# One decoder step on one core: the delta rule's sample stage takes in the gated norm behind it, and the attention's outputs use other PSUM banks

## The reference

```python
# odd layer: one input projection, two head groups, one output projection
o_dn, s_dn = delta_rule(dq, dk, dv, gdec, beta, s_dn)     # 4 heads of 128; one state of 128 x 128 per sample and head
o_dn = rmsnorm(o_dn, dn_norm) * silu(dz)                  # per head, over its 128 features: the gated norm
out = concat([o_sb, o_dn]) @ w_out

# every layer: cross-attention to 256 memory rows, 4 heads of 256
s = q @ mk.T * 256 ** -0.5
o = softmax(s) @ mv                                        # the outputs
x += o @ w_xo
```

## Time and profile before

| | us |
|---|---|
| three runs: median (lowest to highest) | 2115.48 (2109.58 to 2116.85) |
| the profiled execution, its own time | 2111.75 |
| its span, first to last instruction | 2110.0 |
| TensorE busy | 1979.2 (94%) |
| VectorE busy | 1194.9 (57%) |
| ScalarE busy | 504.4 (24%) |
| GpSimd busy | 231.5 (11%) |

### The profile page before, as it was taken

The page is one execution under the profiler, slowest core; times in us unless marked ns, Lnnn a source line. Parts: engine busy times, 40 slices in busy tenths (PEclk is TensorE's granted clock), DMA queues, the critical chain, the costliest instruction groups (busy, mean ns, idle before and its releaser), DMA issues. The chain is left out here.

```text
span 2110.0 us, 40071 instructions
## 1 busy us (share of the span) xinstructions
PE 1979.2 (94%) x17677; PEld 1849.6 (88%) x17677; DVE 1194.9 (57%) x1470; ACT 504.4 (24%) x844; POOL 231.5 (11%) x221
## 2 busy tenths in 40 slices
PE   7999889989889999999999988887898899999999
PEld 6998769879859999999999965576897599999999
DVE  6885575477446555554467446555764365555432
ACT  2222543242232111110021045432422321111000
POOL 3110131021102000001110011021311020000000
PEclk9999899999999999999999999789999999999999
DMA  5222220024442222232222242302345422222321
GB/s 195 82 80 82 86 88 3 4 100 170 166 204 101 90 93 88 98 106 96 76 76 96 72 143 74 115 15 91 131 165 204 176 91 94 86 98 89 110 96 54
DMA packets 55283, 215.44 MB, mean 102 GB/s; under 512 B 6770, under 2 KB 9458, under 8 KB 48626
## 3 DMA queue, kind: packets, MB, share of 16 engines
q1 hardware_dynamic: 55154, 213.59, 28.4%
HBM read 198.07 MB, written 15.50 MB: 101 GB/s over the span
## 5 line engine op out<-in xcount | busy, mean ns | idle before, releaser
L592 PE MATMUL ps<-mx_hi,w_hi 128*128 128x260 f32 x2560 | 520.7, 285 | 17.9 <-DVE w_lo L565 9.6
L592 PE MATMUL ps<-mx_hi,w_lo 128*128 128x260 f32 x2560 | 517.0, 284 | 0.0
L592 PE MATMUL ps<-mx_lo,w_hi 128*128 128x260 f32 x2560 | 516.2, 283 | 0.0
L592 PEld LDWEIGHTS ps<-mx_hi,w_hi 128*128 128x128 f32 x2560 | 396.1, 189 | 22.2 <-DVE w_lo L565 9.8
L592 PEld LDWEIGHTS ps<-mx_hi,w_lo 128*128 128x128 f32 x2560 | 396.2, 189 | 0.0
L592 PEld LDWEIGHTS ps<-mx_lo,w_hi 128*128 128x128 f32 x2560 | 394.9, 189 | 0.0
L563 DVE CAST w_hi<-w 128x1024 fp32r<-128x1024 f32 (+1 forms) x240 | 177.7, 741 | 287.1 <-PE ps L592 285.5
L565 DVE TENSOR_TENSOR w_lo<-w,w_hi 128x1024 fp32r<-128x1024 f32 (+1 forms) x240 | 316.3, 1318 | 8.3
L592 PE MATMUL ps<-hid_hi,w_hi 128*128 128x260 f32 x704 | 141.8, 283 | 0.0
L592 PE MATMUL ps<-hid_hi,w_lo 128*128 128x260 f32 x704 | 141.7, 283 | 0.0
L592 PE MATMUL ps<-hid_lo,w_hi 128*128 128x260 f32 x704 | 141.3, 282 | 0.0
(11 more groups left out here) (513 smaller groups left out, 2780.5 us busy)
## 6 DMA issues: line engine op xcount, KB each, us to landing
w<-in_w_gu SPq DMA_DIRECT2D x88, 512.0 KB, 3.2
w<-in_w_in SPq DMA_DIRECT2D x56, 512.0 KB, 3.2
w<-in_w_down SPq DMA_DIRECT2D x32, 704.0 KB, 4.0
w<-in_w_xkv SPq DMA_DIRECT2D x32, 512.0 KB, 3.3
scr<-in_mem_k SPq DMA_DIRECT2D x10, 1024.0 KB, 7.0
scr<-in_mem_v SPq DMA_DIRECT2D x10, 1024.0 KB, 14.1
w<-in_w_out SPq DMA_DIRECT2D x16, 512.0 KB, 6.0
w<-in_w_xq SPq DMA_DIRECT2D x16, 512.0 KB, 3.3
```

Of the source, the lines that this page charges most:

```text
L592: ins = nc.tensor.matmul(self.ps[:, 2 * (o % 2) + s, 0:b - a], w[:, k, :], v[:, x, a:b], start=first, stop=last)
```

## The change

Two things are edited.

In `attention`, the outputs of heads 0 and 2 stay in banks 4 and 5, those of head 1 go to banks 0 and 1 and those of head 3 to banks 6 and 7. The outputs of heads 1 and 3 wait for the exponentials of heads 2 and 3, which read these banks last; the outputs of head 2 wait for `kept` of head 0. A wait for `kept` of head 1 is put ahead of the samples' values, which write bank 0.

In the delta part, `gated_norm` goes as a stage of its own, and `delta_sample` does its work: ScalarE squares the prompt columns at the stage's start, TensorE sums them beside the sample products, the logarithms and one exponential stand between ScalarE's copies, and the product of gate and `z` moves from VectorE to GpSimd. The 32 sample columns get squares, sums, logarithm and exponential of their own at the end. VectorE's two splits move behind the adds, two low tiles move ahead of them, and `begin` starts after low tile 3. The first half of the key product of unit 7 moves to the end of `delta_chain`.

The diff, without the removed `gated_norm` (printed above with the other functions) and the two new counters:

```diff
...
         score_bank = (0, 6)
+        out_bank = (4, 0, 4, 6)
...
                     pe.wait_ge(self.scalar_out.sem, self.scalar_out.at(h + 1))
-                    if h:
-                        pe.wait_ge(self.vector_out2.sem, self.vector_out2.at(h))
+                    if h % 2:
+                        pe.wait_ge(self.exp_ready.sem, self.exp_ready.at(3 + h // 2))
+                    elif h:
+                        pe.wait_ge(self.vector_out2.sem, self.vector_out2.at(h - 1))
                     for e in range(2):
                         for m in range(2):
-                            ins = nc.tensor.matmul(self.ps[:, 4 + e, :], vm[:, m, (2 * h + e) * P:(2 * h + e + 1) * P],
+                            ins = nc.tensor.matmul(self.ps[:, out_bank[h] + e, :], vm[:, m, (2 * h + e) * P:(2 * h + e + 1) * P],
                                                    pt[h % 2][:, m], start=m == 0, stop=m == 1)
...
                 outputs(2)
+                pe.wait_ge(self.vector_out2.sem, self.vector_out2.at(2))
                 for b0 in KEY_ORDER[0:4]:
...
                     act.wait_ge(self.tensor_out2.sem, self.tensor_out2.at(h + 1))
-                    nc.scalar.activation(self.src[0][:, 2 * h:2 * h + 2, 0:T], self.ps[:, 4:6, :], ACT.Copy).then_inc(
+                    nc.scalar.activation(self.src[0][:, 2 * h:2 * h + 2, 0:T], self.ps[:, out_bank[h]:out_bank[h] + 2, :], ACT.Copy).then_inc(
                         self.source_hi.sem, 1)
...
                     dve.wait_ge(self.source_hi.sem, his + h + 1)
-                    self.dve.tell(nc.vector.tensor_tensor(self.src[1][:, 2 * h:2 * h + 2, 0:T], self.ps[:, 4:6, :],
+                    self.dve.tell(nc.vector.tensor_tensor(self.src[1][:, 2 * h:2 * h + 2, 0:T], self.ps[:, out_bank[h]:out_bank[h] + 2, :],
                                                           self.src[0][:, 2 * h:2 * h + 2, 0:T].bitcast(F32), ALU.subtract),
...
                 output(NC - 1, range(4)).then_inc(self.tensor_out.sem, 1)
+                pe.wait_ge(self.ahead_kept.sem, self.ahead_kept.at(7))
+                self.ahead.product(pe, 7, 7, range(0, 4))
                 self.tensor_out.count += 1
...
         bs = self.cut(self.E_COL + 64, 4, B)
+        o, sg, z = self.o[:, 4:8, :], self.cut(self.ODD_GATES, 4, N), c[:, DZ:DZ + 4]
+        rms = self.cut(self.ODD_GATES + 2080, 4, N)
+        two = lambda t, x: t[:, 2 * x:2 * x + 2]
+        sum_bank = (4, 5, 6, 1)
...
         with self.stage() as block:
-            his = self.take(self.source_hi, 4)
+            his, done = self.take(self.source_hi, KT), self.take(self.source_ready, 4)
+            self.out_leg = self.leg(following, self.src, self.SPANS)
...
                 self.pool.tell(nc.gpsimd.memset(blocks.rearrange("p a h x -> p (a h x)"), 0.0), self.pool_out)
+                pool.wait_ge(self.gate_scalar.sem, self.gate_scalar.at(1))
+                self.pool.tell(nc.gpsimd.tensor_tensor(sg, sg, z, ALU.mult), self.pool_out)
...
             def _(pe):
-                self.ahead.product(pe, 7, 7)
+                def norm_sums(x):
+                    pe.wait_ge(self.squares_ready.sem, self.squares_ready.at(x + 1))
+                    for h in (2 * x, 2 * x + 1):
+                        ins = nc.tensor.matmul(self.ps[:, sum_bank[h], :], self.const("ones"), rms[:, h, 0:T], start=True, stop=True)
+                    ins.then_inc(self.delta_sums.sem, 1)
+
+                self.ahead.product(pe, 7, 7, range(4, KT))
+                norm_sums(0)
                 pe.wait_ge(self.vector_out.sem, self.vector_out.at(1))
...
                 ins.then_inc(self.tensor_out.sem, 1)
+                norm_sums(1)
                 for b0 in range(B):
...
                 pe.wait_ge(self.scalar_out.sem, self.scalar_out.at(2))
+                pe.wait_ge(self.ahead_kept.sem, self.ahead_kept.at(8))
+                pe.wait_ge(self.delta_logs.sem, self.delta_logs.at(2))
                 for half in range(2):
...
                 nc.tensor.transpose(self.ps[:, 2, 0:P], out, self.const("ident")).then_inc(self.tensor_out.sem, 1)
+                pe.wait_ge(self.squares_ready.sem, self.squares_ready.at(3))
+                for h in range(4):
+                    ins = nc.tensor.matmul(self.ps[:, 4, h * B:(h + 1) * B], self.const("ones"), rms[:, h, T:N], start=True, stop=True)
+                ins.then_inc(self.delta_sums.sem, 1)
+                pe.wait_ge(self.source_lo.sem, self.source_lo.at(4))
+                self.begin(pe, self.out_leg, self.OUT_BEGUN)
                 self.tensor_out.count += 4
                 self.tensor_out2.count += 2
+                self.delta_sums.count += 3
...
             def _(act):
+                def log(out, sums, n):
+                    act.wait_ge(self.delta_sums.sem, self.delta_sums.at(n))
+                    self.act.tell(nc.scalar.activation(out, sums, ACT.Ln, bias=self.eps, scale=1.0 / P), self.delta_logs)
+
+                for x in range(2):
+                    self.act.tell(nc.scalar.activation(two(rms, x)[:, :, 0:T], two(o, x)[:, :, 0:T], ACT.Square), self.squares_ready)
                 self.ahead.kept(act, 7, 7)
+                act.wait_ge(self.vector_out.sem, self.vector_out.at(1))
+                self.source_hi_tile(act, 0)
+                log(two(rms, 0)[:, :, 0:T], self.ps[:, 4:6, :], 1)
                 act.wait_ge(self.tensor_out.sem, self.tensor_out.at(1))
...
                               self.scalar_out)
+                self.source_hi_tile(act, 1)
+                act.wait_ge(self.delta_sums.sem, self.delta_sums.at(2))
+                self.act.step(nc.scalar.activation(rms[:, 2, 0:T], self.ps[:, 6, :], ACT.Ln, bias=self.eps, scale=1.0 / P))
+                log(rms[:, 3, 0:T], self.ps[:, 1, :], 2)
                 act.wait_ge(self.tensor_out.sem, self.tensor_out.at(2))
                 self.act.tell(nc.scalar.activation(u, self.ps[:, 0, 0:P], ACT.Copy), self.scalar_out)
+                self.act.step(nc.scalar.activation(rms[:, :, 0:T], rms[:, :, 0:T], ACT.Exp, scale=-0.5))
                 self.gates_on_scalar(DZ, self.ODD_GATES)
-                for t in range(4):
+                for t in range(2, 4):
                     self.source_hi_tile(act, t)
...
                 act.wait_ge(self.tensor_out.sem, self.tensor_out.at(4))
-                self.act.step(nc.scalar.activation(self.o[:, 4:8, T:N],
-                                                   self.ps[:, 2, 0:P].rearrange("p (h x) -> p h x", h=4)[:, :, 0:B], ACT.Copy))
+                self.act.tell(nc.scalar.activation(o[:, :, T:N], self.ps[:, 2, 0:P].rearrange("p (h x) -> p h x", h=4)[:, :, 0:B],
+                                                   ACT.Copy), self.scalar_out)
+                self.act.tell(nc.scalar.activation(rms[:, :, T:N], o[:, :, T:N], ACT.Square), self.squares_ready)
+                log(rms[:, :, T:N], self.ps[:, 4, 0:4 * B].rearrange("p (h b) -> p h b", b=B), 3)
+                self.act.tell(nc.scalar.activation(rms[:, :, T:N], rms[:, :, T:N], ACT.Exp, scale=-0.5), self.scalar_out)
+                for j in range(4):
+                    act.wait_ge(self.source_ready.sem, done + j + 1)
+                    self.source_hi_tile(act, 4 + j)
...
             def _(dve):
+                def low(j):
+                    dve.wait_ge(self.source_hi.sem, his + j + 1)
+                    self.dve.tell(self.source_lo_tile(j), self.source_lo)
+
                 dve.wait_ge(self.pool_out.sem, self.pool_out.at(1))
...
                                                           ALU.mult), self.vector_out)
-                for g in range(2):
-                    self.split(dve, following.at + g)
+                for t in range(2):
+                    low(t)
                 for half in range(2):
...
                     self.dve.tell(ins, self.vector_out2)
-                self.gates_on_vector(dve, DZ, self.ODD_GATES)
-                for t in range(4):
-                    dve.wait_ge(self.source_hi.sem, his + t + 1)
-                    self.dve.step(self.source_lo_tile(t))
+                for g in range(2):
+                    self.split(dve, following.at + g)
+                for t in range(2, 4):
+                    low(t)
+                dve.wait_ge(self.pool_out.sem, self.pool_out.at(2))
+                dve.wait_ge(self.scalar_out.sem, self.scalar_out.at(4))
+                for h in range(4):
+                    ins = nc.vector.scalar_tensor_tensor(sg[:, h], sg[:, h], self.param("dn_norm")[:, 0:1], o[:, h], ALU.mult, ALU.mult)
+                self.dve.step(ins)
+                dve.wait_ge(self.scalar_out.sem, self.scalar_out.at(5))
+                for h in range(4):
+                    nc.vector.tensor_tensor(o[:, h], sg[:, h], rms[:, h], ALU.mult).then_inc(self.source_ready.sem, 1)
+                    if h:
+                        low(3 + h)
+                low(7)
...
         self.delta_sample(L["out1"])
-        self.gated_norm(4, self.ODD_GATES, "dn_norm", L["out1"])
```

(19 more changed lines are left out.)

## The result

| | before | after |
|---|---|---|
| median of 5 runs each (lowest to highest), us | 2115.48 (2109.58 to 2118.72) | 2101.45 (2098.95 to 2105.59) |
| the profiled execution, us | 2111.75 | 2101.45 |
| its span, us | 2110.0 | 2099.7 |
| sample stage's first matmul to the out loop's first, us | 38.95 | 34.16 |
| out loop's first matmul to the mark behind the second attention, us | 188.51 | 184.99 |

What follows compares the result with a forecast made beforehand. TensorE, busy 94% of the span, was taken as the bound. Attention −6.9 and merged stage −4.4 gave −11.3 us: 2100.5 from the profiled execution, 2104.2 from the median; forecast 2103, own range 2098 to 2108.

Steps and rivals of the forecast that it cites:

- The attention edit: Attention stages: new output banks remove all 4 TensorE waits on kept, −6.9 us; lower bound of the gain −4.9.
- rival (c): Attention: other waits of the same length replace those on kept, leaving −4.4 us, 2111.1; chance 0.10.
- Sample stage, TensorE's start: Sample stage: half the key product moves out, prompt sums move in; outer products start at about 1464.7 instead of 1464.31, +0.4.
- VectorE's order: Sample stage: splits go behind the adds, two low tiles ahead; adds end at 1470.8 and not 1473.24, −2.4 us.
- GpSimd's product: Sample stage: gate's product moves to GpSimd at 4.5 us; VectorE is spared 2.33 but its splits lose 3.5.
- The sum: Attention −6.9 and merged stage −4.4 give −11.3 us for the run; forecast time 2103 us.
- the hold: Sample stage: VectorE's instructions with SBUF inputs stand during GpSimd's product; splits lose 3.5 us, 4.5 if adds are held too.
- Rival (a): Sample stage: GpSimd's product does not hold VectorE or falls into its pauses; stage −8.0, run 2100.5; chance 0.17.
- The end of the stage: Sample stage's end: separate norm work gone, VectorE ends at 1488.2, begun part just covered; −4.4 us.
- rival (b): Merged stage gains nothing: TensorE's begun part later and colder, VectorE's row longer; only −6.9, 2108.6; chance 0.13.
- (d): Rival: begun part starts at half clock, which lasts far into the out projection; slower, above 2121.8; chance 0.05.

Runs made afterwards that it cites:

- whole_key_product: Changed kernel with the whole key product of unit 7 back in the sample stage; median 2108.34 us, ratio to before 0.9959, stage 35.92 us.
- attention_only: Kernel before with only the attention edit's new banks and waits; median 2106.9 us, ratio to before 0.9963.
- splits_first: Changed kernel with VectorE's two splits ahead of the adds again; median 2102.36 us, ratio to before 0.9926, stage 33.21 us.
- gate_in_chain: Changed kernel with the gate's sigmoid and product moved into the delta chain, the product on VectorE; median 2097.61 us, ratio to before 0.9920, stage 30.78 us.
- gate_on_vector: Changed kernel with the product of gate and z back on VectorE, behind low tile 3; median 2100.41 us, ratio to before 0.9943, stage 33.15 us.
- sigmoid_first: Changed kernel with ScalarE's sigmoid ahead of the big exponential, so GpSimd's product starts earlier; median 2100.28 us, ratio to before 0.9941, stage 32.27 us.
- merge_only: Changed kernel with the attention edit undone and all else kept; median 2107.75 us, ratio to before 0.9974, stage 34.18 us.

## Why the prediction was right

**The attention edit.** Right, in mechanism and size: 6.9 us forecast, 3.5 and 4.0 measured by the marks, the wait on `kept` gone in both layers, and no wait before the transposes of head 3, so rival (c) fell. It was close: in the first layer the scaled weights of head 3 were done at 614.38, 0.2 us ahead of the transposes at 614.60 (0.4 forecast). What it did not see is that head 1's move alone would do it.

**Sample stage, TensorE's start.** The rest of the key product took 1.96 us (1.8 forecast), each pair of sums 1.9 (1.84), and the outer products started 10.04 us after the stage's start (10.4). That the other half is free under ScalarE's copy held: from the chain's last outputs to the stage's start it is 2.8 us in after as in whole_key_product. The 5.37 us as the price of the whole product hold for one of two clocks only: attention_only has 5.29 behind the same wait, whole_key_product 3.69.

**VectorE's order.** The adds ended 16.33 us after the stage's start (16.5 forecast). But that the splits' move is a gain of 2.4 us holds only for the adds. What left the place ahead of them came back under GpSimd's product; with the splits left there the stage was 0.95 us shorter. The sum was right because the hold was in it as a term of its own.

**GpSimd's product.** 4.59 us (4.5 forecast), 3.4 lost by VectorE (3.5), and the adds not held. Rival (a) fell.

**The end of the stage.** VectorE's last low tile was done 33.5 us after the start, and the loop came 0.67 later: 34.16 (34.6 forecast), so −4.8 and not −4.4. What the sum names in half a sentence, that the norm stage's own start, sums and exponentials are gone, is what pays for the splits and the hold behind the adds. The begun part started at half clock, took 8.2 us (8 to 8.7 forecast) and ended at 1485.53, 0.29 before VectorE at 1485.82: rival (b) missed by that much. The loop ran at 1.00, so (d) fell.

**The sum.** −11.3 forecast, −12.3 in the edited places, −14.0 between the medians with an interval of −18.0 to −9.7. That the median came within 1.5 us of 2103 is in part luck: the time was laid between 2100.5 and 2104.2, the places fell 1.0 us short in the sum, and the traces differ by 2.0 in code that was not edited.

## What to carry to other kernels

Work handed to GpSimd was free for VectorE here only under the adds, which read one operand from PSUM (4.99 us with it beside them and without); copies and subtractions from SBUF stood until it was done. So look for such a place for it, and look at what slides beneath it when something else is moved. Before shortening one engine's row at a stage's end, read when the other one ends: three of the edits here that shortened VectorE's row met the end of TensorE's begun part (splits_first, gate_in_chain), or left TensorE standing for 3.15 us, with the next loop's start at a clock of 0.72 (gate_on_vector). Where several tiles share a buffer in turn, one tile with a buffer of its own can free the whole chain.

## What the runs showed of the hardware

- The stand before the out loop and the clock over its first 6 us, in layer 1: behind 0.45, 0.59, 0.97, 1.34 and 1.42 us the loop ran at 1.00 (splits_first, gate_in_chain, after, sigmoid_first, before), behind 1.84 and 3.15 us at 0.72 (whole_key_product, gate_on_vector). In layer 0, behind 3.66 to 4.20 us, it ran at 0.50 to 0.76, and not in the order of the stands: behind 3.85 us at 0.75 in merge_only and at 0.53 in sigmoid_first.
- When the clock falls differs between executions of the same instructions: the second half of the outputs took 1.94 us in after and 1.08 in sigmoid_first, behind the same wait of 1.43 us. Behind the same wait of 2.38 us the key product's 16 instructions ran at 0.68 and 0.69 in before and attention_only, and at 1.00 in whole_key_product.
- GpSimd's product of 128x2080 took 4.59 to 4.63 us whether VectorE's adds or a held split stood beside it; VectorE does it in 2.33.
